# A state-space recurrence taken over four time steps, with four tiles a round

## The reference

```
lam_dt = lam * dt;  a_bar = exp(lam_dt)
b_bar = ((a_bar - 1.0) / lam)[:, :, None] * b          # 64 groups, 64 complex states, 16 channels
bu = einsum('gph,bcgh->bcgp', b_bar, u)
xs[t] = a_bar * xs[t-1] + bu[t]                        # the recurrence, complex
y = einsum('ghp,bcgp->bcgh', c, xs).real + d_g * u
z = gelu(y) @ w_glu + b_glu
out = z[..., :D_MODEL] * sigmoid(z[..., D_MODEL:])
```

## Time and profile before

| | |
|---|---|
| time, median of 3 runs | 2096.45 us (2095.57 to 2096.51) |
| the profiled execution | 2094.85 us |
| its span, first to last instruction | 2093.1 us |
| mean granted clock of PE over the span | 0.947 |
| busy: PE, PEld, DVE, ACT | 92%, 80%, 66%, 51% |
| the state-space stage's loop | 1657.95 to 1762.82 us of the span |

### The profile page before, as it was taken

The page is one execution under the profiler, slowest core; times in us unless marked ns, Lnnn a source line. Parts: engine busy times, 40 slices in busy tenths (PEclk is TensorE's granted clock), DMA queues, the critical chain, the costliest instruction groups (busy, mean ns, idle before and its releaser), DMA issues.

```text
span 2093.1 us, 29528 instructions
## 1 busy us (share of the span) xinstructions
PE 1916.8 (92%) x11986; PEld 1681.6 (80%) x11986; DVE 1371.9 (66%) x1888; ACT 1072.7 (51%) x1583; POOL 0.2 (0%) x4
## 2 busy tenths in 40 slices
PE   7998999999999989998998999979998367899996
PEld 5887677777777769997887999869997345799995
DVE  4635999999999966554334655436554996265552
ACT  3334988888888854443334444334443222254442
POOL 0000000000000000000000000000000000000000
PEclk9999999999999999999999999989999556999999
DMA  6326999999999955542343554235542100545520
GB/s 245 115 91 235 350 366 359 367 359 365 361 363 357 364 196 208 182 151 76 123 127 148 197 186 180 88 121 185 183 173 87 48 1 21 191 165 186 186 84 20
DMA packets 45661, 408.71 MB, mean 195 GB/s; under 512 B 4800, under 2 KB 10432, under 8 KB 11344
## 3 DMA queue, kind: packets, MB, share of 16 engines
q1 hardware_dynamic: 40688, 398.86, 51.0%
q10 hardware_dynamic: 4832, 7.90, 1.2%
HBM read 405.66 MB, written 1.08 MB: 194 GB/s over the span
## 4 chain that ended last, share of the span: by engine, by line
PE 67%; DVE 28%; ACT 3%; issue 1%; DMA 0%; DVEq 0%; ACTq 0%; SPq 0%
PE wk L1558 25%; DVE ws_moe L1049 15%; PE acc L1536 12%; PE wk L358 7%; PE wk L1003 3%; PE wk L1814 3%; PE wk L364 2%; PE wk L927 2%; PE acc L893 2%; PE wk L313 1%; PE acc L710 1%; DVE rstd L285 1%; PE acc L1843 1%; DVE sq L1116 1%; DVE scr_ssm L2252 1%
## 5 line engine op out<-in xcount | busy, mean ns | idle before, releaser
L1049 DVE TENSOR_TENSOR ws_moe<-ring,ws_moe 128x1024 fp32r<-128x1024 f32 x384 | 447.3, 1213 | 5.5 <-ACT ws_moe L1042 5.2
L1042 ACT ACTIVATE ws_moe<-ring 128x1024 fp32r<-128x1024 f32 x384 | 384.3, 1051 | 4.9 <-PE wk L1003 2.2
L1558 PE MATMUL wk<-hx,gu 128*128 128x256 f32 x2112 | 277.2, 289 | 5.0 <-DVE hx L1574 4.7
L1558 PEld LDWEIGHTS wk<-hx,gu 128*128 128x128 f32 x2112 | 265.9, 195 | 10.2 <-DVE hx L1574 6.9
L1003 PE MATMUL wk<-ws_moe,xp_moe 128*128 128x512 f32 x1024 | 268.3, 404 | 1.6 <-DVE xp_moe L1071 1.6
L1536 PE MATMUL acc<-hh_ffn,dn_ffn 128*128 128x256 f32 x2112 | 267.1, 283 | 0.0
L1558 PE MATMUL wk<-hx,gu_ffn 128*128 128x256 f32 x2112 | 260.6, 283 | 0.0
L1536 PEld LDWEIGHTS acc<-hh_ffn,dn_ffn 128*128 128x128 f32 x2112 | 259.5, 192 | 0.0
L1558 PEld LDWEIGHTS wk<-hx,gu_ffn 128*128 128x128 f32 x2112 | 256.6, 192 | 0.0
L1515 ACT ACTIVATE hT<-hT 128x256 f32<-128x256 f32 x88 | 36.8, 419 | 370.3 <-DVE hT L1590 370.3
L1003 PEld LDWEIGHTS wk<-ws_moe,xp_moe 128*128 128x128 f32 x1024 | 187.1, 188 | 43.6 <-issue 2.8
(11 more groups left out here) (333 smaller groups left out, 2294.1 us busy)
## 6 DMA issues: line engine op xcount, KB each, us to landing
ring<-in_u_moe SPq DMA_DIRECT2D x129, 1536.0 KB, 8.3
ring<-in_u_ffn SPq DMA_DIRECT2D x88, 1536.0 KB, 6.2
ring<-in_u_qkv SPq DMA_DIRECT2D x12, 1024.0 KB, 5.0
ring<-in_u_ple SPq DMA_DIRECT2D x8, 1280.0 KB, 5.6
ring<-in_u_in SPq DMA_DIRECT2D x9, 1024.0 KB, 5.0
ring<-in_u_glu SPq DMA_DIRECT2D x8, 1024.0 KB, 5.1
ring<-in_u_out SPq DMA_DIRECT2D x4, 1024.0 KB, 4.9
ring<-in_u_o SPq DMA_DIRECT2D x4, 1024.0 KB, 5.0
```

The lines of the kernel that those rows point to most:

```text
L1042: e.activation(WS[:, n % NWS, 0, :], piece(x), ACT.Copy).then_inc(s.m_hi, 1)
L1049: e.tensor_tensor(WS[:, n % NWS, 1, :], piece(x), WS[:, n % NWS, 0, :].bitcast(F32), SUB).then_inc(s.m_lo, 1)
L1558: m = e.matmul(b[:, a * T:(a + 1) * T], gu_of(c, f)[:, x, a * 1024 + k * 128:a * 1024 + (k + 1) * 128], HX[:, y, k, :], start=k == 0 and a ...
```

## The change

The recurrence is taken over four steps (LS = 4) in place of two, with four tiles a round (NQ = 8 rounds, QT = 64 groups of steps). DVE's tensors keep 512 elements. The four scans become one over all 512, with a decay tensor `rm` that ACT fills in each round (r4 = |a|^4, zero where a tile or a part begins). The drive has four input steps: 32 products with N 64, spread over the four row tiles of PE. wk's four banks now hold one round's drives. The states have four output steps: 32 products with N 64 (or 63), over the four column tiles, and six products for each tile lead directly from an input step to the same or a later output step (`between_pe`), with factors of 96 columns.

The factors a^d B (d = 1 to 3) and C a^d w (d = 0 to 3) are formed by DVE in compact form, without the zeros of the other group, 512 elements each; ACT spreads each into its place (E4 with a mask of constants, CC into memory that GpSimd has set to zero). PE's `abc` products fold two groups' rows into 64 columns. ACT issues its loads in pairs between its steps instead of all six ahead. The scratch memory moves ahead of two buffers that the feed-forward parts use, and shares their space. The constants grow by 66 columns.

```diff
...
+        scr4, = area("_ssm", ("scr", [128, 26784], F32))
         GU0 = sb("gu0", [128, 2, 2048], F32R)
...
+        S4 = Scr(scr4, 26784, 8192)
+        r_, r4, fr, ar, ai, wre, wim, tA, tB, tC, tE = (S4.get(32) for _ in range(11))
+        LS, NQ = 4, 8
...
+        rm = [S4.get(4, 2, QT) for _ in range(2)]
...
+        pr, pq, ww = ([S4.get(4, 2, QT) for _ in range(2)] for _ in range(3))
+        xx = [S4.get(4, 2, QT) for _ in range(3)]
...
+        eB = [[part(2 * n + z, 8) for z in range(2)] for n in range(2)]
+        cO = [[part(4 + 2 * n + z, 32) for z in range(2)] for n in range(2)]
+        tmp = part(8, 8), part(8, 32)
+        E4 = [[scr4[:, 1024 * (2 * d + z):1024 * (2 * d + z + 1)].rearrange("p (k n) -> p k n", k=8) for z in range(2)] for d in range(LS)]
+        BTre, BTim = (sq[:, 4 * n:4 * n + 4, :].rearrange("p a t -> p (a t)").rearrange("p (a b) -> p a b", a=32) for n in range(2))
...
+            x = ap.rearrange("p (j s) -> p s j", s=LS)
+            return [x[:, i, :] for i in range(LS)]
...
+        def decay_act(e, m):
+            if m >= 2:
+                e.wait_ge(s.W, m - 1)
+            for x in range(4):
+                c = e.activation(rm[m % 2][:, x, :, :], cs("scanm", 0, 2 * QT).rearrange("p (z t) -> p z t", z=2), ACT.Copy,
+                                 scale=r4[:, 4 * m + x:4 * m + x + 1])
+            c.then_inc(s.rm, 1)
         def ssm_act(e):
             leave(e)
             squares_act(e, "ssm", ("ffn", 2))
             root(e, "ssm")
             enter(e, fence_of["ssm"])
...
             e.activation(tA, sm("log_dt"), ACT.Exp).then_inc(s.dtx, 1)
+            for z, n in enumerate(("cBre", "cBim")):
+                e.dma_start(eB[0][z], A[n]).then_inc(s.ld_cb, 16)
             e.wait_ge(s.tB, 1)
             e.activation(r_, tB, ACT.Exp).then_inc(s.rx, 1)
+            for z, n in enumerate(("cCre", "cCim")):
+                e.dma_start(cO[0][z], A[n]).then_inc(s.ld_cc, 16)
             e.wait_ge(s.fr, 1)
             e.activation(wim, fr, ACT.Abs).then_inc(s.scl, C.up())
             e.activation(tC, fr, ACT.Sin, scale=TWO_PI * (1 - 1e-7))
             e.wait_ge(s.scl, C.n)
             e.activation(tB, wim, ACT.Sin, scale=-TWO_PI, bias=cs("halfpi")).then_inc(s.sn, 1)
+            for z, n in enumerate(("sBre", "sBim")):
+                e.dma_start(E4[0][z], A[n]).then_inc(s.ld_e, 16)
             e.wait_ge(s.ab, 1)
...
+            e.wait_ge(s.ccz, 2)
+            for z, src in enumerate((ar, ai)):
+                for g in range(2):
+                    r, c = half(g)
+                    e.activation(CC[z][r, 0, :, c], src[r, :].rearrange("p (a o) -> p a o", o=1).broadcast_to([64, 32, 16]),
+                                 ACT.Copy).then_inc(s.aw, 1)
+            for x, n in ((BTre, "sBTre"), (BTim, "sBTim")):
+                e.dma_start(x, A[n]).then_inc(s.ld_bt4, 16)
             tables_act(e, 0)
             tables_act(e, 1)
+            for d in range(1, LS):
+                for z in range(2):
+                    e.wait_ge(s.eB, 2 * d - 1 + z)
+                    for g in range(2):
+                        e.activation(E4[d][z][:, :, 64 * g:64 * g + 64], eB[d % 2][z], ACT.Copy,
+                                     scale=cs("half", g, g + 1)).then_inc(s.eX, 1)
+            decay_act(e, 0)
+            decay_act(e, 1)
+            e.wait_ge(s.ccz, 4)
+            for d in range(LS):
+                for z in range(2):
+                    e.wait_ge(s.cw, 2 * d + z + 1)
+                    for g in range(2):
+                        r, c = half(g)
+                        e.activation(CC[z][r, d, :, c], cO[(d + 1) % 2][z][r, :, :], ACT.Copy).then_inc(s.cX, 1)
             e.wait_ge(s.cb, 1)
...
+            for n in range(2):
+                m = e.activation(CB[:, 4 * n:4 * n + 4, :], acc[:, 2 + n, 0:384].rearrange("p (a b) -> p a b", a=4), ACT.Copy)
+            m.then_inc(s.cbd, 1)
+            for m in range(2, NQ):
                 tables_act(e, m)
+                decay_act(e, m)
             for j in range(4):
                 e.wait_ge(s.y_, 2 * j + 2)
...
+        def drive_pe(e, q):
+            if q:
+                e.wait_ge(s.vfree, q)
+            for z in range(2):
+                for d in range(LS):
+                    for x in range(4):
+                        m = e.matmul(drives[:, x, z, :], E4[d][z][rows(x), q, :], steps(hT[rows(x), q, :])[LS - 1 - d],
+                                     start=z == 0 and d == 0, stop=d == LS - 1, skip_group_check=True)
+            m.then_inc(s.vfull, 1)
+        def between_pe(e, q):
+            for i in range(LS - 1):
+                for o in range(i, LS - 1):
+                    for x in range(4):
+                        y = steps(acc[rows(x), q // 2, q % 2 * T:(q % 2 + 1) * T])[o]
+                        e.matmul(y, CB[rows(x), q, 32 * (o - i):32 * (o - i) + 32], steps(hT[rows(x), q, :])[i],
+                                 start=q % 2 == 0 and i == 0 and o == 0, stop=False, skip_group_check=True)
+        def states_pe(e, q):
+            e.wait_ge(s.W, q + 1)
+            X = xx[q % 3]
+            for o in (LS - 1, *range(LS - 1)):
+                for z in range(2):
+                    for x in range(4):
+                        y = steps(acc[rows(x), q // 2, q % 2 * T:(q % 2 + 1) * T])[o]
+                        last = o == LS - 1
+                        m = e.matmul(y if last else y[:, 1:QT], CC[z][:, 0 if last else o + 1, 4 * q + x, :],
+                                     X[:, x, z, :] if last else X[:, x, z, 0:QT - 1], start=False, stop=z == 1, skip_group_check=True)
+            m.then_inc(s.drive, 1)
...
+            for n in range(2):
                 b = bank_in(e, K("abc", n))
...
+                e.wait_ge(s.aw, 2 * n + 2)
+                for k in range(8):
+                    m = e.matmul(b[:, 64 * k:64 * k + 64], CC[n][:, 0, 4 * k:4 * k + 4, :].rearrange("p a t -> p (a t)"), cs("fold"),
+                                 start=True, stop=True)
                 m.then_inc(s.filled, 1)
...
             h_tile(e, "ssm")
             for i in range(4):
                 e.wait_ge(freed[i], before_loop[i])
+            e.wait_ge(s.ld_e, 32)
+            e.wait_ge(s.eX, 12)
             drive_pe(e, 0)
...
             acc_in(e, "ssm")
...
+            e.wait_ge(s.ld_bt4, 32)
+            e.wait_ge(s.cX, 12)
+            for k in range(8):
+                for z, BT in enumerate((BTre, BTim)):
+                    for x in range(4):
+                        m = e.matmul(acc[rows(x), 2 + k // 4, 96 * (k % 4):96 * (k % 4) + 96], BT[:, 4 * k + x, :], CC[z][:, 0:3, 4 * k + x, :],
+                                     start=k % 4 == 0 and z == 0, stop=z == 1, skip_group_check=True)
             m.then_inc(s.cb, 1)
...
+            e.wait_ge(s.cX, 16)
             e.wait_ge(s.cbd, 1)
...
+            for q in range(NQ):
+                if q + 1 < NQ:
+                    drive_pe(e, q + 1)
+                between_pe(e, q)
+                states_pe(e, q)
+            e.wait_ge(s.vfree, NQ)
...
             e.tensor_tensor(fr, fr, wre, SUB).then_inc(s.fr, 1)
             lr, li = sm("lam_re"), sm("lam_im")
...
+            R, I = (bank_out(e, K("abc", n))[:, :].rearrange("p (a t) -> p a t", a=8) for n in range(2))
+            e.wait_ge(s.ld_cb, 32)
+            for d in range(1, LS):
+                (xr, xi), (yr, yi) = eB[(d - 1) % 2], eB[d % 2]
+                if d == 3:
+                    e.wait_ge(s.eX, 4)
+                own(e.tensor_tensor(t, I, xi, MUL))
+                own(e.tensor_tensor(yr, R, xr, MUL))
+                e.tensor_tensor(yr, yr, t, SUB).then_inc(s.eB, 1)
+                e.wait_ge(s.eB, 2 * d - 1)
+                m = e.tensor_tensor(t, I, xr, MUL)
+                if d == 3:
+                    m.then_inc(freed[K("abc", 1) % 4], 1)
+                    e.tensor_tensor(yi, R, xi, MUL).then_inc(freed[K("abc", 0) % 4], 1)
+                    bank_read(e, K("abc", 0))
+                else:
+                    own(e.tensor_tensor(yi, R, xi, MUL))
+                e.tensor_tensor(yi, yi, t, ADD).then_inc(s.eB, 1)
+                e.wait_ge(s.eB, 2 * d)
+            t = tmp[1]
+            wr3, wi3, ar3, ai3 = (x.rearrange("p (a o) -> p a o", o=1).broadcast_to([128, 32, 16]) for x in (wre, wim, ar, ai))
+            e.wait_ge(s.ld_cc, 32)
+            for d in range(LS):
+                (xr, xi), (yr, yi) = cO[d % 2], cO[(d + 1) % 2]
+                if d >= 2:
+                    e.wait_ge(s.cX, 4 * (d - 1))
+                own(e.tensor_tensor(t, xi, ai3 if d else wi3, MUL))
+                own(e.tensor_tensor(yr, xr, ar3 if d else wr3, MUL))
+                e.tensor_tensor(yr, yr, t, ADD if d else SUB).then_inc(s.cw, 1)
+                e.wait_ge(s.cw, 2 * d + 1)
+                if d:
+                    own(e.tensor_tensor(t, xr, ai3, MUL))
+                    own(e.tensor_tensor(yi, xi, ar3, MUL))
```

(41 more changed lines are left out.)

189 lines of the change are left out of this document (39 added, 150 removed).

## The result

The changed kernel takes 2061.3 us (median of four runs, 2059.1 to 2062.4) where the kernel before takes 2096.0 beside it: a ratio of 0.983, with an interval of 0.982 to 0.985. The forecast was 2063. The profiled execution took 2061.33, its span 2059.5 us, 33.6 less than before.

A forecast was written before the change was run, and what follows sets the result against it. DVE bounds the loop before, PE's relay the new one. Round 1 at 1675.05, six rounds of 7.7 us, last output and states put L358 33.5 us earlier; less 0.2: 2063 us, the likeliest case's own range 2056 to 2070, high 2076.

The forecast's parts named there:

- What bounds the loop before: State-space loop of the kernel before: DVE sets its 16 rounds, 6.44 us each, at granted clock 0.50.
- DVE's terms: DVE in the new loop: scan of 512 at 1.13 us, own work 6.28 us a round, 6.68 with a skip.
- The drive and the relay: New loop: output, states, then drive follow one another, 7.7 us a round, above DVE's 6.3 to 6.7; 58%.
- D: Drive in each round: 16 x 0.213 us, plus filling, tail and the way to DVE: 3.9 us.
- S: States' products in each round: 16 x 0.107 us plus 0.13 for the change of tile shape: 1.84 us.
- the rival of pairs: Drive: row tiles overlap in pairs only, D grows by 3.4 us in seven rounds: 2087 us; chance 10%.
- the slower one: Drive: row tiles' weight loads go one at a time, 13.6 us a drive: 2134 us; chance 3%.
- the denser PE gets 2.4 GHz: Loop: higher clock, or cheaper 32-row loads, leave DVE the bound: 2053 us, 2050 with a faster preparation; chance 22%.
- The preparation: Before the loop: longer DVE chain reaches the loop 9.6 us later, at 1667.5; DVE's second round begins at 1675.05.
- From the last round to the gate products: Loop's end: last output 6.1 us after its round's start, then states and change of shape 1.95 us, then L358.
- Outside the stage: Kernel's start: constants larger by 66 columns delay PE's first product by 0.2 us at most.
- the last case: Late GpSimd clear or longer preparation puts 5 to 15 us before a working loop: 2068 to 2078 us; chance 7%.

The follow-up runs named there:

- the tile order: Changed kernel with all eight drive products of one row tile issued before those of the next: 2108.6 us (one run).
- the half weight columns: Changed kernel whose drive loads and multiplies only 64 of its 128 weight columns, so the output is wrong: 2053.6 us.
- the early output: Changed kernel with DVE forming a round's output at that round's end, not behind the next round's first two products: 2055.5 us.
- the shifted kernels: Kernel before with one 1024-element DVE product of the preparation done twice, or three times: ratios 1.0016 and 1.0025.
- the wide drive: Changed kernel with the drive's 32 products given 128 moving columns in place of 64, each column twice: 2057.6 us.

## Why the prediction was right

The number was right within 2 us, partly because errors of 5 us on either side met.

*What bounds the loop before; DVE's terms.* Right. The scan costs 1.14 from start to start (1.13 forecast), a round of DVE's own work 6.29 (6.28), 6.68 with a skip (6.68).

*The drive and the relay.* The mechanism was right at half clock, shown by the tile order, the half weight columns and the early output: D, from PE's start to DVE's, 3.76 (3.9), S from start to start 1.85 (1.84), a round 7.54 (7.7); the rival of pairs and the slower one are out. The Trainium skill's figure that the prediction set against its row, some 107 ns for a load of 128 columns, is not what the drive shows at half clock, 0.213; at full clock the step of 0.117 leaves room for it. What the prediction missed of the hardware is the floor of such steps; it did no harm, since with 64 moving columns at half clock it is hidden under the load.

*The clock in the loop.* This step failed in part. The rival "the denser PE gets 2.4 GHz" got 22% as a whole, when it came true for parts: drive 1, then rounds 4 and 5. It is worth 1.6 us at drive 1 (2.27 for 3.9), of which 0.5 are lost again because DVE's own first round then ends last, and 2.0 in rounds 4 and 5 (6.70 and 6.68 for 7.7; the other 0.6 of the rounds' gain are the four of 7.54). From round 1 to 7 the loop took 43.55 us, not 46.2. That part of the loop got the higher clock was luck: nothing in the prediction says when.

*The preparation.* 1.3 us too long: 0.7 before the loop, 0.4 in the between factors and 0.2 in their way out. The mis-sized term before the loop is ACT's queue: its loads do not delay its copies, since it issued them while it was reading a table or copying. The copies began 8.95 us after the norm's reciprocal (1630.14), as in the earlier trace rows (8.96), not 0.6 later. PE's 32 products (7.06) and the 18 and 24 products (12.67 and 17.43 us) came as worked out, DVE's start on them 2.2 later than before, not 2.9, which is the same 0.7; the between factors took 4.85, not 5.3. GpSimd's clear took 7 us and was done at 1624.5.

*From the last round to the gate products.* 8.02 us, forecast 8.05.

Together: 1.3 in the preparation, 1.1 at drive 1, 2.7 in the rounds are the 5.1 us by which the stage did better.

*Outside the stage.* Here the forecast had 0.2 us for the constants and nothing else, and this is the step that failed. PE's first product came at 9.66 (9.41 to 9.66 in nine traces with the larger constants, 9.19 to 10.16 in four without: the 0.2 can't be told from the spread); but in this execution the clock then rose late, half until 25.0 in place of 22.8, and the front was 2.1 us longer. In the other traces the front was 0.0 to 2.7 us longer than that of before, and the 2.7 is the kernel before itself with one product twice: this part is chance. The 2.9 us behind the stage are not: falls of the clock behind PE's idle times cost 1.69 and 3.04 us there (13.63 and 40.33 us between the norms' reciprocals, 11.94 and 37.29 before), of which an earlier rise at the gate products and just behind them gives 1.7 back. The prediction took the part behind the stage as it stood in the one trace of before; the shifted kernels show that it hung on the place of two idle times.

*The range.* Two slips that moved nothing: the top is given as the last case's 2076, where that case reads 2078, and the slower case's limit of 8 us a drive is 8.6 by its own terms (33 us in seven rounds on 3.9).

## What to carry to other kernels

Price a tiled fp32 product with few moving columns by its weight load at the clock that the stage really has, and look whether its steps have a floor that the clock doesn't move; then walk the relay between two engines instruction by instruction: moving one DVE instruction a round took 4.4 us off a stage of 105. Where a stage shortens, look at the idle times of TensorE behind it: falls of the clock behind two of them cost up to 4.7 us here, or nothing, so a change of 0.1% in the total can't be judged by the total; compare the stage's own length.

## What the runs showed of the hardware

- Steps of four fp32 records on four row tiles, with moving columns from every fourth place in memory, come no faster than 0.12 us with 64 moving columns (with 32, 64 or 128 weight columns) and 0.23 with 128, at either clock. The states' steps on four column tiles, with columns side by side, don't have this floor (16 steps of 64 columns in 1.09 us at full clock, 1.92 at half). Which of the two makes it was not tested.
- On one row tile a record with 128 weight columns follows the last after 0.213 us at 1.2 GHz, with 64 moving columns as with 32; its product of up to 128 columns fits beside the load (0.227 a step in the wide drive). With 64 weight columns over four tiles the drive stands on the floor. The Trainium skill, page "TensorE: Matmul & The Clock Gate", section "LDWEIGHTS (loading the stationary operand)", says that a load's time goes by its columns and not its rows. The run with half the columns bears out the first (3.69 to 2.12 us), and 0.213 us for 32 rows beside 0.21 for 128 in the earlier trace rows, both at half clock, the second.
- More work per product can be faster, even on the relay that sets the round: with twice the moving columns in the drive the granted clock was 1.00 through the loop where it had been 0.50 in most of it, the drive cost 3.93 us for 3.69, the states 1.09 for 1.92, and the stage was 1.5 us shorter.
- The same idle times of 2.1 and 3.0 us cost the full clock in one kernel and not in another in which the first of them comes 0.33 us earlier, counted from the stage's norm.
